# A third residual buffer, and routing of the next tile begun at the tile's first four tokens with its selection dealt out over 21 fours

## The chip, the cores and the metric

The kernel runs on one core of one Trainium2 chip, in one launch. The metric is device time in microseconds; a run's time is that of the whole program. The kernel before took 4234.45 us (median of 3 runs, 4230.75 to 4238.12).

## The reference

One inference step of a streaming encoder of one layer, with 1024 prompt rows and 8 x 16 sample rows of width 1024, all fp32. Two head groups of attention, an output projection, then a retrieval feed-forward over 16384 single-neuron experts (PEER). The change touches the last only:

```
def peer_block(xb):                                       # 128 tokens, 8 heads
    q  = (xb @ w_query).reshape(128, 8, 2, 128)
    s  = einsum('thpd,hpkd->thpk', q, sub_keys)           # two halves of 128 keys per head
    sv, si = top_k(s, 16)                                 # best 16 of each half
    cand = sv[:, :, 0, :, None] + sv[:, :, 1, None, :]    # 16 x 16 sums
    cidx = si[:, :, 0, :, None] * 128 + si[:, :, 1, None, :]
    fv, fi = top_k(cand.reshape(...), 16)                 # best 16 sums of a head
    eidx = take_along_axis(cidx, fi)                      # 8 x 16 = 128 experts a token
    g = softmax(fv)
    a = einsum('thkd,td->thk', expert_u[eidx], xb)
    w = g * gelu(a)
    return einsum('thk,thkd->td', w, expert_v[eidx])
h = h + peer(rms_norm(h, norm2_g));  y = rms_norm(h, norm_f_g)
```

## The kernel before

The program has two stages. The first does the attention of nine tiles of 128 rows (eight of the prompt, one of the samples) and leaves the residual rows h in a scratch tensor in HBM. The second, from about 1.1 ms on, is the feed-forward, and the change lies wholly in it.

**One token at a time.** A tile's experts are fetched token by token: the 128 experts of one token are one gather of 128 rows (partitions) x 2048 floats, u and v side by side, 1 MB, issued by GpSimd (L1040) into a ring of ten buffers. GpSimd issues gathers of four buffers when the four tokens that held them have been weighed (semaphore `four_used`, L1039). There are 32 "fours" in a tile, numbered f = 0 to 31.

**What a four does.** TensorE spreads the token's normed row over all partitions into PSUM (`spread_x`, L1264, from split bf16 rows x3, two tokens ahead of the dots). VectorE multiplies the u half with it and sums (`dot`, L1120), giving 128 scores. After four dots ScalarE takes one gelu (L1099) and multiplies with the gates (L1105). TensorE then weighs the v halves, accumulating in two PSUM banks over the whole tile (`weigh`, L1276). Then GpSimd issues four more gathers.

**Routing of the next tile** runs inside the current tile's fours, cut into steps that tables place: `PE_AT`, `ACT_AT` and `DVE_AT` (L59 to L76) give for each four the steps of TensorE, ScalarE and VectorE; each engine runs its queue strictly in that order, so a step that waits holds what is behind it. The steps of tile t + 1:

- norm: ScalarE squares the residual rows in `hb` and takes the root (L1050 to L1054), VectorE inverts it (L120 on) and forms x2 (L1139).
- split: VectorE cuts x2 into three bf16 parts (L1144 to L1152); SP copies these in 12 DMAs to x3 (L993).
- x2T: TensorE transposes x2 (L1288), ScalarE copies it out.
- q (k, l), k and l from 0 to 3: TensorE, 8 block products each (L1298); ScalarE copies four of them at once (L1061).
- keys (k): TensorE (L1307), then ScalarE's copy of the scores (L1069).
- halves (k, l): VectorE, the best 16 of 128 (`top16`, L1123); sums (k); best (k, h): the best 16 of 50 sums; experts (k, h): the expert numbers (L1193 to L1203). In all 16 + 4 + 8 + 8 steps a tile, the "selection".
- shift, gates, turn, turned: softmax of the gates, and the transposed lists that GpSimd and ScalarE read.

On TensorE the first step of a four stands amid the four's spreads and the others behind its weighing (L1325 to L1335). On VectorE the i-th step of a four stands behind its i-th dot. ScalarE's steps stand ahead of the four's gelu.

**End of a tile**, inside the next one: collect (VectorE adds PSUM to `hb`, at four 1; weighing waits for it), squares (ScalarE, L1079, at four 2), finish (VectorE, L1226, at four 3). SP then stores the block, waits for that, loads the block after next into the same one of two `hb` buffers (L996 to L1007), and goes on to the copies of the split rows (`spread`, L987).

Of the kernel before, what the change touches and what calls it, by code (L numbers as in the profile page):

```python
# [55 lines left out]
COLLECT_AT, SQUARES_AT, FINISH_AT = 1, 2, 3  # L56
# [3 lines left out]
PE_AT = {5: [("x2T",)], 23: [("turn",)], 14: [("keys", 3)]}  # L60
for k in range(4):
    PE_AT.setdefault(6 + 2 * k, [])
    if k:
        PE_AT[6 + 2 * k] += [("keys", k - 1)]
    PE_AT[6 + 2 * k] += [("q", k, 0), ("q", k, 1)]
    PE_AT[7 + 2 * k] = [("q", k, 2), ("q", k, 3)]
ACT_AT = {4: [("norm",)], 6: [("x2T",)], 8: [("q", 0)], 9: [("keys", 0)], 10: [("q", 1)], 11: [("keys", 1)],
          12: [("q", 2)], 13: [("keys", 2)], 14: [("q", 3)], 15: [("keys", 3)], 22: [("gates",)], 24: [("turned",)]}
ACT_ORDER = [s for f in sorted(ACT_AT) for s in ACT_AT[f]]
DVE_AT = {4: [("norm",)], 6: [("split",)], 21: [("shift",)], 22: [("gates",)], 24: [("turned",)]}  # L70
for k in range(4):
    pieces = [("halves", k, l) for l in range(4)] + [("sums", k), ("best", k, 0), ("best", k, 1)]
    pieces += [("experts", k, 0), ("experts", k, 1)]
    for i in range(3):
        DVE_AT[9 + 3 * k + i] = pieces[3 * i:3 * i + 3]
# [62 lines left out]
def build(nc, ins, outs):  # L138
# [6 lines left out]
    with ctx:  # L145
        def sem(name):
            return ctx.enter_context(nc.semaphore(name))
# [753 lines left out]
        hb = [carve(D) for _ in range(2)]  # L901
# [16 lines left out]
        c_left = carve(CAND)  # L918
# [18 lines left out]
        h_in = [sem(f"h_in{p}") for p in range(2)]  # L937
# [40 lines left out]
        with nc.Block() as block:  # L978

            @block.sync  # L980
            def _(sp):
                sp.dma_start(hb[0], h_dram[0:P, :]).then_inc(h_in[0], 16)
                sp.dma_start(g2_bc, g2[0:1, :].broadcast_to([P, D])).then_inc(bc_in, 16)
                sp.dma_start(gf_bc, gf[0:1, :].broadcast_to([P, D])).then_inc(bc_in, 16)
                sp.dma_start(hb[1], h_dram[P:2 * P, :]).then_inc(h_in[1], 16)

                def spread(t):  # L987
                    sp.wait_ge(split_ready, 3 * t + 3)
                    if t >= 2:
                        sp.wait_ge(xb_ready, SLOTS * (t - 1))  # L990
                    for c in range(3):
                        for g in range(4):
                            sp.dma_start(x3[t % 2][32 * c:32 * c + 32, g, :], parts3[c][32 * g:32 * g + 32, :])\  # L993
                              .then_inc(x3_in[t % 2], 16)

                def store(t):  # L996
                    sp.wait_ge(y_ready, t + 1)
                    sp.dma_start(y_p[t * P:(t + 1) * P, :] if t < NT_PROMPT else y_s, hb[t % 2]).then_inc(y_stored, 16)

                spread(0)  # L1000
                for t in range(NT):
                    if t >= 1:
                        store(t - 1)
                        if t + 1 < NT:
                            sp.wait_ge(y_stored, 16 * t)
                            sp.dma_start(hb[(t + 1) % 2], h_dram[(t + 1) * P:(t + 2) * P, :])\
                              .then_inc(h_in[(t + 1) % 2], 16)  # L1007
                    if t + 1 < NT:
                        spread(t + 1)
                store(NT - 1)  # L1010
                sp.wait_ge(y_stored, 16 * NT)

# [97 lines left out]
            def _(dve):  # L1110
# [22 lines left out]
                def route(t, step, k=0, h=0):  # L1133
                    p = t % 2
                    hs = slice(QSP * k, QSP * (k + 1))
                    if step == "norm":
                        dve.wait_ge(rms2_ready, t + 1)
                        invert_rms(dve, ch, rstd2[:, 0:1], ss2[:, 0:1], newton2, D)
                        dve.scalar_tensor_tensor(out=x2, in0=hb[p], scalar=rstd2[:, 0:1], in1=g2_bc,  # L1139
                                                 op0=ALU.mult, op1=ALU.mult).then_inc(x2_ready, 1)  # L1140
                    if step == "split":
# [4 lines left out]
                        if t >= 2:  # L1146
                            dve.wait_ge(ssf_ready, t - 1)
# [73 lines left out]
                def collect(t):  # L1221
                    dve.wait_ge(four_used, FOURS * (t + 1))
                    dve.tensor_tensor(hb[t % 2], PS[:, ACC:ACC + 2, :].rearrange("p a b -> p (a b)"), hb[t % 2], ALU.add)\
                       .then_inc(acc_free, 1)

                def finish(t):  # L1226
# [3 lines left out]
                    dve.scalar_tensor_tensor(out=hb[t % 2], in0=hb[t % 2], scalar=rstd2[:, 1:2], in1=gf_bc,  # L1230
# [22 lines left out]
            def _(pe):  # L1253
# [68 lines left out]
                for t in range(NT):  # L1322
                    for f in range(FOURS):
# [4 lines left out]
                        for step, *k in steps[:1]:  # L1328
                            route(t + 1, step, *k)
# [4 lines left out]
                        for step, *k in steps[1:]:  # L1334
                            route(t + 1, step, *k)  # L1335
# [63 lines left out]
```

## Time and profile before

| | us |
|---|---|
| runs, median of 3 | 4234.45 |
| profiled execution | 4222.83 |
| its span, first to last instruction | 4221.0 |
| TensorE busy | 2997.1 (71%) |
| VectorE busy | 2380.9 (56%) |
| ScalarE busy | 731.7 (17%) |
| GpSimd busy | 1181.9 (28%) |
| gathers, share of the 16 DMA engines over the span | 70.6% |

The shares are means over two unlike stages. In the second stage the slices of the page show DMA at 9 or 8 tenths nearly throughout and between 350 and 422 GB/s. To see what a four costs, the trace is cut at the gelus: stretch f of a tile runs from the start of the gelu of four f to that of four f + 1, and so holds the weighing of four f and the dots of four f + 1. DMA share is the mean busy share of the core's 16 DMA engines. The granted clock of TensorE is given as a share of 2.4 GHz.

### The profile page before, as it was taken

Reading aid. Unit: us, or ns where it says so; the run is one execution under the profiler, and the core shown is the slowest. Engines: PE = TensorE matmul, PEld = TensorE weight load, DVE = VectorE, ACT = ScalarE, POOL = GpSimd, SP = SyncE. Lnnn points to the kernel's source line nnn. Section 1 sums busy time; section 2 is a strip of 40 time slices with the busy share of each in tenths; the row PEclk is TensorE's granted clock in tenths of the full one; section 3 lists DMA queues with packets and bytes.
Section 4 is the critical chain, followed back from the end, with each engine's and each line's share of the span. In section 5 each row is a group of like instructions: output and inputs, shape, how many; then the busy total and the mean of one; then the engine's idle time right before and its main releaser. Section 6 shows DMA issues by size and latency. Waiting matters only on the chain.

```text
span 4221.0 us, 39656 instructions
## 1 busy us (share of the span) xinstructions
PE 2997.1 (71%) x13023; PEld 1218.1 (29%) x13023; DVE 2380.9 (56%) x6206; ACT 731.7 (17%) x2364; POOL 1181.9 (28%) x1330
## 2 busy tenths in 40 slices
PE   8999999996376666667657666666766765766665
PEld 4555555575041132123114113112311311311111
DVE  2333333324668469558657756855865774684544
ACT  2333333311111111111111111111111111111111
POOL 1001000000223333333432333333333333233332
PEclk9999999957587687777668768767767866877676
DMA  4000000231699999998999999999899999999998
GB/s 177 10 10 10 15 15 19 72 134 33 253 372 379 422 392 365 414 396 357 409 405 369 391 421 371 367 422 394 350 413 402 366 400 422 368 372 421 421 422 350
DMA packets 193573, 1276.81 MB, mean 302 GB/s; under 512 B 22640, under 2 KB 26608, under 8 KB 44528
## 3 DMA queue, kind: packets, MB, share of 16 engines
q0 software_dynamic: 165888, 1208.03, 70.6%
q1 hardware_dynamic: 27504, 66.63, 4.5%
q8 instruction: 81, 1.33, 0.1%
q14 instruction: 100, 0.82, 0.1%
HBM read 1255.17 MB, written 12.32 MB: 300 GB/s over the span
## 4 chain that ended last, share of the span: by engine, by line
DMA 28%; DVE 16%; PE 16%; issue 8%; ACT 4%; POOL 4%; DVEq 0%; POOLq 0%; SPq 0%; ACTq 0%
DMA arena<-in_experts,arena 25%; PE PS L1276 12%; DVE arena L1120 6%; POOL arena L1040 4%; ACT arena L1105 3%; PE PS L1298 3%; DVE arena L1198 1%; DVE arena L1195 1%; DVE arena L1201 1%; DMA out<-arena 1%; DMA arena<-h_scratch 1%; PE PS L1264 1%; DVE arena L1131 1%; DVE arena L1126 1%; DVE arena L1129 1%
## 5 line engine op out<-in xcount | busy, mean ns | idle before, releaser
L1120 DVE CUSTOM_DVE_ANT_0 arena<-arena,PS 128x1024 f32<-128x1024 f32 x1152 | 1393.1, 1220 | 999.5 <-DMA arena<-in_experts,arena 544.4
L1040 POOL DMA_INDIRECT arena<-in_experts,arena x1152 | 1106.3, 960 | 2090.6 <-PE PS L1276 1728.9
L1264 PE MATMUL PS<-arena 96*128 96x512 bf16 x2304 | 831.1, 468 | 983.4 <-DVE arena L1120 978.9
L1276 PE MATMUL PS<-arena 128*32 128x512 f32 x4608 | 955.0, 974 | 75.2 <-ACT arena L1105 35.5
L1264 PEld LDWEIGHTS PS<-arena 96*128 96x128 bf16 x2304 | 170.7, 105 | 1712.4 <-DVE arena L1120 1374.4
L1099 ACT ACTIVATE arena<-arena 128x4 f32<-128x4 f32 x288 | 59.2, 205 | 2405.1 <-DVE arena L1120 2395.9
L1276 PEld LDWEIGHTS PS<-arena 128*32 128x32 f32 x4608 | 166.8, 153 | 662.6 <-issue 384.4
L1298 PEld LDWEIGHTS PS<-arena 128*128 128x128 f32 x2304 | 291.6, 205 | 95.8 <-issue 88.5
L1298 PE MATMUL PS<-arena 128*128 128x128 f32 x2304 | 304.6, 291 | 1.1 <-ACT arena L1057 1.1
L739 PE MATMUL PS<-arena 128*128 128x512 f32 (+1 forms) x720 | 290.0, 556 | 3.8 <-ACT arena L471 2.9
L1105 ACT ACTIVATE arena<-arena 128x1 f32<-128x1 f32 x1152 | 244.9, 283 | 9.6
L422 POOL COPY arena<-arena 128x512 f32<-128x512 f32 x36 | 22.2, 616 | 687.4 <-POOLq L111 685.8
L739 PEld LDWEIGHTS PS<-arena 128*128 128x128 f32 x720 | 134.4, 192 | 132.7 <-issue 129.4
L719 PE MATMUL PS<-ident,arena 128*128 128x128 f32 x741 | 129.2, 306 | 45.5 <-ACT arena L521 24.2
L606 DVE TENSOR_TENSOR arena<-PS,arena 128x256 f32<-128x256 f32 x64 | 27.2, 424 | 197.2 <-PE PS L767 195.0
L811 PE MATMUL PS<-arena 128*128 128x512 f32 x288 | 129.1, 607 | 11.8 <-DVE arena L582 11.8
L521 ACT ACTIVATE arena<-arena 128x256 f32<-128x256 f32 (+1 forms) x128 | 85.6, 669 | 250.0 <-DVE arena L612 250.0
L719 PEld LDWEIGHTS PS<-ident,arena 128*128 128x128 f32 x741 | 98.9, 161 | 74.4 <-issue 30.7
L791 PE MATMUL PS<-arena 128*128 128x128 f32 (+1 forms) x640 | 100.3, 311 | 0.0
L610 DVE CUSTOM_DVE_ANT_0 arena<-arena 128x256 f32<-128x256 f32 (+1 forms) x128 | 83.8, 655 | 24.7 <-DVEq L111 24.7
L125 DVE TENSOR_SCALAR arena<-arena 128x1 f32<-128x1 f32 (+1 forms) x36 | 7.2, 199 | 156.3 <-ACT arena L1053 70.4
L1120 DVE DVE_READ_ACCUMULATOR2_ANT arena<- 128x1 f32 x1152 | 94.9, 82 | 0.0
(168 smaller groups left out, 2146.4 us busy)
## 6 DMA issues: line engine op xcount, KB each, us to landing
arena<-in_experts,arena POOLq DMA_INDIRECT x1152
arena<-in_w_in SPq DMA_DIRECT2D x4, 2048.0 KB, 16.0
arena<-in_w_query SPq DMA_DIRECT2D x8, 1024.0 KB, 5.7
arena<-arena SPq DMA_DIRECT2D x108, 64.0 KB
h_scratch<-arena SPq DMA_DIRECT2D x9, 512.0 KB, 2.6
arena<-h_scratch SPq DMA_DIRECT2D x9, 512.0 KB, 7.8
out<-arena SPq DMA_DIRECT2D x9, 512.0 KB, 8.0
arena<-in_x_prompt SPq DMA_DIRECT2D x8, 512.0 KB, 3.9
```

Source lines behind the costliest of these rows:

```text
L521: act.activation(sc[n % 2][:, 0:w], sc[n % 2][:, 0:w], ACT.Exp, bias=nm[:, n:n + 1], accum_out=den[:, n:n + 1]).then_inc(e_ready, 1)
L610: ch.mark(dve.tensor_tensor_reduce(s, s, bias, 1.0, floor, ALU.add, ALU.max, m_sb[:, n:n + 1]))
L719: return pe.transpose(PS[:, bank, k * P:(k + 1) * P], src, ident)
L739: mm = pe.matmul(PS[:, UNIT, 0:w], xT[:, j, :], w_in_sb[:, j, 512 * c:512 * c + w], start=(j == 0), stop=(j == KD - 1))
L791: mm = pe.matmul(PS[:, OA_BANK, cols], pT[n % 2][:, k, :], v_win[:, k, cols], start=(k == 0), stop=(k == A_BLK - 1))
L811: mm = pe.matmul(PS[:, 6 + c, :], oT[:, k, :], w_out_sb[:, k, 512 * c:512 * c + 512], start=(k == 0), stop=(k == KD - 1))
L1040: pool.indirect_dma_start(out=uv[r], out_offset=None, in_=experts, in_offset=bass.IndirectOffsetOnAxis(ap=expert_T[t % 2][:, tok:tok + 1], ...
L1105: act.activation(wz[n % 2][:, g, 31:32], a_gelu[n % 2][:, g:g + 1], ACT.Copy, scale=gate_T[t % 2][:, tok:tok + 1]).then_inc(wgt_ready, 1)
L1120: dve.tensor_tensor_reduce(uv[r][:, 0:D], uv[r][:, 0:D], xb(n), 1.0, 0.0, ALU.mult, ALU.add, a_dot[(n // 4) % 2][:, n % 4:n % 4 + 1]).then ...
L1264: mm = pe.matmul(PS[:, 2 + 2 * (n % 2) + c, :], pick[0:96, j:j + 1].broadcast_to([96, P]), x3[t % 2][0:96, g, 512 * c:512 * c + 512], star ...
L1276: mm = pe.matmul(PS[32 * g:32 * g + 32, ACC + c, :], wz[n % 2][:, g, 31 - f:63 - f], uv[r][:, D + 512 * c:D + 512 * c + 512], start=(f == ...
L1298: mm = pe.matmul(PS[:, Q_BANK, l * P:(l + 1) * P], w_query_sb[:, j, c:c + P], x2T[:, j, :], start=(j == 0), stop=(j == KD - 1))
```

## The change

There are three residual buffers instead of two; the load of a block is issued two tiles ahead. On SP the copies of the split rows stand ahead of the store. Routing starts at four 0 (norm), 1 (split, transposes) and 2 (first products). The products of a k come at fours 2 + 5k and 3 + 5k, the scores at 4 + 5k, always behind the weighing. ScalarE copies the products at 4 + 5k and the scores at 5 + 5k. VectorE's 36 selection steps are dealt by fixed lengths over fours 5 to 25, an experts step directly behind its best step. Squares move to four 4, finish to four 5. The squares' scratch is x2 instead of the score buffer, with another wait; one small scratch shares a buffer.

```
-COLLECT_AT, SQUARES_AT, FINISH_AT = 1, 2, 3
+COLLECT_AT, SQUARES_AT, FINISH_AT = 1, 4, 5
-PE_AT = {5: [("x2T",)], 23: [("turn",)], 14: [("keys", 3)]}
+PE_AT = {1: [("x2T",)], 27: [("turn",)]}
+ACT_AT = {0: [("norm",)], 2: [("x2T",)], 26: [("gates",)], 28: [("turned",)]}
 for k in range(4):
-    PE_AT.setdefault(6 + 2 * k, [])
-    if k:
-        PE_AT[6 + 2 * k] += [("keys", k - 1)]
-    PE_AT[6 + 2 * k] += [("q", k, 0), ("q", k, 1)]
-    PE_AT[7 + 2 * k] = [("q", k, 2), ("q", k, 3)]
-ACT_AT = {4: [("norm",)], 6: [("x2T",)], 8: [("q", 0)], 9: [("keys", 0)], 10: [("q", 1)], 11: [("keys", 1)],
-          12: [("q", 2)], 13: [("keys", 2)], 14: [("q", 3)], 15: [("keys", 3)], 22: [("gates",)], 24: [("turned",)]}
+    PE_AT[2 + 5 * k] = [("q", k, 0), ("q", k, 1)]
+    PE_AT[3 + 5 * k] = [("q", k, 2), ("q", k, 3)]
+    PE_AT[4 + 5 * k] = [("keys", k)]
+    ACT_AT[4 + 5 * k] = [("q", k)]
+    ACT_AT[5 + 5 * k] = [("keys", k)]
-DVE_AT = {4: [("norm",)], 6: [("split",)], 21: [("shift",)], 22: [("gates",)], 24: [("turned",)]}
-for k in range(4):
-    pieces = [("halves", k, l) for l in range(4)] + [("sums", k), ("best", k, 0), ("best", k, 1)]
-    pieces += [("experts", k, 0), ("experts", k, 1)]
-    for i in range(3):
-        DVE_AT[9 + 3 * k + i] = pieces[3 * i:3 * i + 3]
+SELECT_AT, SELECT_FOURS = 5, 21
+STEP_LENGTH = {"halves": 4, "sums": 6, "best": 3, "experts": 6}
+SELECTION = []
+for k in range(4):
+    SELECTION += [("halves", k, l) for l in range(4)]
+    SELECTION += [("sums", k), ("best", k, 0), ("experts", k, 0), ("best", k, 1), ("experts", k, 1)]
+DVE_AT = {0: [("norm",)], 1: [("split",)]}
+select_length = sum(STEP_LENGTH[s[0]] for s in SELECTION)
+before = 0
+for s in SELECTION:
+    DVE_AT.setdefault(SELECT_AT + before * SELECT_FOURS // select_length, []).append(s)
+    before += STEP_LENGTH[s[0]]
+DVE_AT[SELECT_AT + SELECT_FOURS - 1].append(("shift",))
+DVE_AT[SELECT_AT + SELECT_FOURS] = [("gates",)]
+DVE_AT[28] = [("turned",)]
...
-        hb = [carve(D) for _ in range(2)]
+        hb = [carve(D) for _ in range(3)]
-        c_left = carve(CAND)
+        c_left = s_left[:, 0:CAND]
...
                 spread(0)
                 for t in range(NT):
+                    if t + 1 < NT:
+                        spread(t + 1)
                     if t >= 1:
                         store(t - 1)
-                        if t + 1 < NT:
+                        if t + 2 < NT:
                             sp.wait_ge(y_stored, 16 * t)
-                            sp.dma_start(hb[(t + 1) % 2], h_dram[(t + 1) * P:(t + 2) * P, :])\
-                              .then_inc(h_in[(t + 1) % 2], 16)
-                    if t + 1 < NT:
-                        spread(t + 1)
+                            sp.dma_start(hb[(t + 2) % 3], h_dram[(t + 2) * P:(t + 3) * P, :])\
+                              .then_inc(h_in[(t + 2) % 3], 16)
...
                 def squares(t):
                     act.wait_ge(acc_free, t + 1)
-                    act.wait_ge(halves_done, 4 * min(t + 2, NT))
-                    act.activation(s_flat, hb[t % 2], ACT.Square, accum_out=ss2[:, 1:2]).then_inc(ssf_ready, 1)
+                    act.wait_ge(split_ready, 3 * min(t + 3, NT))
+                    act.wait_ge(x2T_psum, min(t + 3, NT))
+                    act.activation(x2, hb[t % 3], ACT.Square, accum_out=ss2[:, 1:2]).then_inc(ssf_ready, 1)
...
                     if step == "split":
-                        if t >= 2:
-                            dve.wait_ge(ssf_ready, t - 1)
...
                         spread_x(4 * n + 2)
                         spread_x(4 * n + 3)
-                        for step, *k in steps[:1]:
-                            route(t + 1, step, *k)
                         spread_x(4 * n + 4)
                         spread_x(4 * n + 5)
                         weigh(n, 0)
                         weigh(n, 1)
-                        for step, *k in steps[1:]:
+                        for step, *k in steps:
                             route(t + 1, step, *k)
```

The dealing gives VectorE these steps of the selection, k / l or h:

```
four  5 halves 0/0 0/1      four 12 sums 1                  four 19 best 2/1, experts 2/1
four  6 halves 0/2 0/3      four 13 best 1/0, experts 1/0   four 20 halves 3/0
four  7 sums 0, best 0/0    four 14 best 1/1, experts 1/1   four 21 halves 3/1 3/2
four  8 experts 0/0         four 15 halves 2/0              four 22 halves 3/3, sums 3
four  9 best 0/1, exp. 0/1  four 16 halves 2/1 2/2          four 23 best 3/0
four 10 halves 1/0 1/1      four 17 halves 2/3, sums 2      four 24 experts 3/0, best 3/1
four 11 halves 1/2 1/3      four 18 best 2/0, experts 2/0   four 25 experts 3/1
```

## Rows read from the trace of the kernel before

**Rows 1.** Head of the page.
```profile
span 4221.0 us, 39656 instructions
```

**Rows 2.** Tiles 0, 4, 8: length; busy PE, PEld, DVE, ACT, POOL; clock; DMA share; GB/s.
```profile
1111.90:1454.40 342.50, 232.89 (x1064) 75.22 (x1064) 226.94 (x576) 45.84 (x179) 123.68 (x128) 0.74 0.98 393
...
2499.20:2849.10 349.90, 230.17 (x1066) 72.55 (x1066) 229.66 (x584) 49.81 (x184) 123.33 (x128) 0.73 0.97 390
...
3895.00:4206.60 311.60, 199.39 (x742) 35.73 (x742) 155.41 (x256) 36.63 (x161) 110.59 (x118) 0.69 1.00 415
```

**Rows 3.** The same of tile 4: its stretches 3-5, 6-7, 8-13, 14-21, 22-31.
```profile
2529.90:2564.60 34.70, 19.53 (x95) 6.08 (x96) 19.91 (x35) 8.07 (x21) 11.76 (x12) 0.71 0.95 386
2564.60:2588.90 24.30, 16.82 (x109) 8.89 (x106) 9.84 (x16) 2.72 (x12) 7.50 (x8) 0.91 1.02 365
2588.90:2668.50 79.60, 60.90 (x361) 33.28 (x361) 61.32 (x201) 9.50 (x37) 23.26 (x24) 0.82 0.89 355
2668.50:2748.30 79.80, 50.61 (x192) 9.50 (x192) 71.48 (x220) 11.77 (x44) 30.48 (x31) 0.67 0.96 383
2748.30:2849.10 100.80, 63.52 (x242) 11.42 (x242) 49.35 (x81) 10.71 (x52) 39.08 (x42) 0.69 1.01 421
```

**Rows 4.** The same of single stretches: vector-bound, the two behind it, a quiet one.
```profile
2720.10:2732.50 12.40, 6.51 (x24) 1.15 (x24) 11.99 (x25) 1.02 (x6) 4.61 (x4) 0.64 0.97 388
2732.50:2740.70 8.20, 6.67 (x25) 1.26 (x26) 4.89 (x10) 1.10 (x6) 2.51 (x3) 0.66 0.97 381
2740.70:2748.30 7.60, 5.59 (x24) 1.10 (x24) 5.46 (x11) 3.89 (x8) 3.39 (x5) 0.77 1.00 417
...
2788.10:2798.00 9.90, 6.21 (x24) 1.12 (x24) 4.92 (x8) 1.02 (x5) 3.75 (x4) 0.67 1.02 423
```

**Rows 5.** Timeline of a quiet four: start, us, engine, line, operation, idle before.
```profile
2789.20 3.62 PE L1276 MATMUL PS<-arena 128*32 128x512 f32 x16
...
2792.75 1.04 PE L1264 MATMUL PS<-arena 96*128 96x512 bf16 x4
...
2793.13 0.94 POOL L1040 DMA_INDIRECT arena<-in_experts,arena  x1 [5.41 <-PE PS L1276]
```

**Rows 6.** Timeline around the norm step of tile 4.
```profile
2531.58 0.35 SPq L1006 DMA_DIRECT2D arena<-h_scratch  x1
...
2539.37 1.06 ACT L1051 ACTIVATE arena<-arena 128x1024 f32<-128x1024 f32 x1 [8.38 <-DMA arena<-h_scratch]
2540.54 1.28 ACT L1053 ACT_TABLE_LOAD   x1
...
2542.14 1.28 ACT L1099 ACT_TABLE_LOAD   x1
2542.16 0.15 DVE L125 TENSOR_SCALAR arena<-arena 128x1 f32<-128x1 f32 x1 [8.93 <-ACT arena L1053]
```

**Rows 7.** Timeline of TensorE and VectorE: two product blocks behind a weighing, twice.
```profile
2590.01 3.64 PE L1276 MATMUL PS<-arena 128*32 128x512 f32 x16
2593.59 4.35 PE L1298 MATMUL PS<-arena 128*128 128x128 f32 x32
...
2599.75 1.22 DVE L1120 CUSTOM_DVE_ANT_0 arena<-arena,PS 128x1024 f32<-128x1024 f32 x1 [3.98 <-issue]
...
2616.01 3.17 PE L1276 MATMUL PS<-arena 128*32 128x512 f32 x16 [0.31 <-ACT arena L1105]
...
2623.82 1.22 DVE L1120 CUSTOM_DVE_ANT_0 arena<-arena,PS 128x1024 f32<-128x1024 f32 x1 [2.23 <-PE PS L1264]
```

**Rows 8.** Timeline: scores on TensorE, their copy, first and last operation of a selection.
```profile
2583.86 1.13 PE L1307 MATMUL PS<-arena 128*128 128x128 f32 x8
...
2642.62 0.56 ACT L1069 COPY arena<-PS 128x512 f32<-128x512 f32 x1
...
2591.24 0.29 DVE L1124 MAX8 arena<-arena 128x8 f32<-128x128 f32 x1
...
2592.63 0.28 DVE L1131 FIND_INDEX8 arena<-arena 128x8 uint32<-128x128 f32 x1
```

More of the change, by code:

```diff
@@ L936, in build @@
         bc_in = sem("bc_in")
-        h_in = [sem(f"h_in{p}") for p in range(2)]
+        h_in = [sem(f"h_in{p}") for p in range(3)]
         rank_ready = sem("rank_ready")
@@ L984, in _ @@
                 sp.dma_start(gf_bc, gf[0:1, :].broadcast_to([P, D])).then_inc(bc_in, 16)
-                sp.dma_start(hb[1], h_dram[P:2 * P, :]).then_inc(h_in[1], 16)
+                for t in range(1, 3):
+                    sp.dma_start(hb[t], h_dram[t * P:(t + 1) * P, :]).then_inc(h_in[t], 16)
                 def spread(t):
@@ L997, in store @@
                     sp.wait_ge(y_ready, t + 1)
-                    sp.dma_start(y_p[t * P:(t + 1) * P, :] if t < NT_PROMPT else y_s, hb[t % 2]).then_inc(y_stored, 16)
+                    sp.dma_start(y_p[t * P:(t + 1) * P, :] if t < NT_PROMPT else y_s, hb[t % 3]).then_inc(y_stored, 16)
                 spread(0)
                 for t in range(NT):
+                    if t + 1 < NT:
+                        spread(t + 1)
                     if t >= 1:
                         store(t - 1)
-                        if t + 1 < NT:
+                        if t + 2 < NT:
                             sp.wait_ge(y_stored, 16 * t)
-                            sp.dma_start(hb[(t + 1) % 2], h_dram[(t + 1) * P:(t + 2) * P, :])\
-                              .then_inc(h_in[(t + 1) % 2], 16)
-                    if t + 1 < NT:
-                        spread(t + 1)
+                            sp.dma_start(hb[(t + 2) % 3], h_dram[(t + 2) * P:(t + 3) * P, :])\
+                              .then_inc(h_in[(t + 2) % 3], 16)
                 store(NT - 1)
@@ L1049, in route @@
                     if step == "norm":
-                        act.wait_ge(h_in[p], 16 * (t // 2) + 16)
-                        act.activation(x2, hb[p], ACT.Square, accum_out=ss2[:, 0:1]).then_inc(ss2_ready, 1)
+                        act.wait_ge(h_in[t % 3], 16 * (t // 3) + 16)
+                        act.activation(x2, hb[t % 3], ACT.Square, accum_out=ss2[:, 0:1]).then_inc(ss2_ready, 1)
                         act.wait_ge(ss2_ready, t + 1)
@@ L1138, in route @@
                         invert_rms(dve, ch, rstd2[:, 0:1], ss2[:, 0:1], newton2, D)
-                        dve.scalar_tensor_tensor(out=x2, in0=hb[p], scalar=rstd2[:, 0:1], in1=g2_bc,
+                        dve.scalar_tensor_tensor(out=x2, in0=hb[t % 3], scalar=rstd2[:, 0:1], in1=g2_bc,
                                                  op0=ALU.mult, op1=ALU.mult).then_inc(x2_ready, 1)
@@ L1222, in collect @@
                     dve.wait_ge(four_used, FOURS * (t + 1))
-                    dve.tensor_tensor(hb[t % 2], PS[:, ACC:ACC + 2, :].rearrange("p a b -> p (a b)"), hb[t % 2], ALU.add)\
+                    dve.tensor_tensor(hb[t % 3], PS[:, ACC:ACC + 2, :].rearrange("p a b -> p (a b)"), hb[t % 3], ALU.add)\
                        .then_inc(acc_free, 1)
@@ L1229, in finish @@
                     ch.restart()
-                    dve.scalar_tensor_tensor(out=hb[t % 2], in0=hb[t % 2], scalar=rstd2[:, 1:2], in1=gf_bc,
+                    dve.scalar_tensor_tensor(out=hb[t % 3], in0=hb[t % 3], scalar=rstd2[:, 1:2], in1=gf_bc,
                                              op0=ALU.mult, op1=ALU.mult).then_inc(y_ready, 1)
```

## The prediction

> **What bounds the kernel now.** Times in the profile are of one execution: span 4221.0 us, execution 4222.8 us, 11.6 us under the median of the three runs, 4234.45 [rows 1]. I forecast for the profiled execution and add 11.6 at the end.
>
> I read the slices of the page first (the DMA line is at 8 or 9 from the twelfth on: the expert stage), then stretches cut at the tiles. A tile with routing of the next one in it takes 342.5 us (the first), then seven tiles from 1454.4 to 3895.0, a mean of 348.7. The last tile, which routes nothing, needs 311.6 us for 31 of its 32 fours and runs at 415 GB/s [rows 2]. So the gathers of expert rows are the floor, and routing puts some 25 us per tile on top. The reader is to see in [rows 3] where: one tile cut at the gelus of its fours (stretch f runs from the gelu of four f to that of four f+1). In a quiet four the DMA share is 1.01, 423 GB/s, 9.9 us [rows 4], so 32 fours are 316.8 us. Stretches 6 and 7 take 24.3 us at share 1.02 but 365 GB/s: the twelve copies that make the split token rows are then in the DMA engines, which costs 24.3 - 19.8 = 4.5 us. Store and load of a residual block, 1.05 MB at 423 GB/s, are 2.5 us. Floor: 316.8 + 4.5 + 2.5 = 323.8. Above it tile 4 (349.9) loses 26.1: 1.0 in stretches 0 to 2 (the 30.7 us that the others leave); 34.7 - 29.7 - 2.5 = 2.5 in 3 to 5; 79.6 - 59.4 = 20.2 in 8 to 13, where the projection is on TensorE and the DMA share falls to 0.89; 0.6 in 14 to 21; 1.8 in 22 to 31. The mean tile loses 348.7 - 323.8 = 24.9.
>
> How much lateness is free? Four gathers are issued when the weighing matmuls of a four end, 5 us after its gelu (gelu 2788.10, weighing 2789.20, its follower 2792.75, first issue 2793.13) [rows 4, 5]. A four that comes late starves the DMA only once it has eaten the transfers still queued. When the consumer was the brake and then is let go, it catches up by what lay ready: after the last vector-bound stretch (2720.10, 12.4 us) the next two take 8.2 and 7.6 instead of 9.9, together 4.0 us [rows 4]. So up to about 4.0 us of lateness costs nothing, and what exceeds it is lost for good. This is my main tool: I follow lateness L from four to four, and cut it at 4.0.
>
> **The change part by part.**
>
> *Third buffer, norm moved from four 4 to four 0.* Before, the load of the next residual block is issued at 2531.58, after the store of the old one, and ScalarE's Square starts only at 2539.37; VectorE waits 8.93 us for the norm and its dots stand still [rows 6]. With a third buffer the block is there four fours earlier. Of the 18.1 us stretch only 2.5 us were lost (above), since the ring covered the rest. Late next: at four 0 the norm's Square, table load and root (2.7 us, [rows 6]) start after the last weights, 1.0 us behind the gelu, so VectorE has them at 3.8; its own part, six steps on one column and a pass, is under two dots' time (2.4), so it is through at 6.2, with 9.9 - 6.2 = 3.7 us for the three dots left: nothing lost. On SP the copies of the split rows now go ahead of the store; the store waits for the finish at four 5 anyway, so nothing is late there.
>
> *Split and collect at four 1.* behind one dot (over at 2.4) VectorE adds collect and the split, five passes over 128x1024 at a dot's 1.2 or less: 8.4 with them, 12.0 with the three dots left, instead of 9.9: L = 2.1, gone in the next four, which can do 9 us where the data's pace is 12.15 (next sentence but one). The scratch of the final squares goes to another buffer and its wait is on steps long done: nothing. The twelve copies move with the split to about fours 2 and 3; their 4.5 us stay, and slow the data there, so pace is 12.15 in these two.
>
> *Projection spread out.* The same matmuls: two blocks behind the weighing of fours 2+5k and 3+5k, keys behind 4+5k (k = 0 to 3). Before, fours 6 to 13 had two blocks each, one of them often amid the spreads. The price of two blocks behind a weighing stands in the trace: weighing from 2590.01, 32 matmuls from 2593.59 for 4.35, third dot of the next four at 2599.75; in a second case weighing 2616.01, third dot 2623.82 [rows 7]. Gelu to weighing 1.1, weighing to third dot 7.8 or 9.7, two more dots 2.4: the next four takes 11.3 to 13.3; I take the middle, 12.3 (A). There are eight A: fours 3, 4, 8, 9, 13, 14, 18, 19.
>
> *Squares at four 4.* ScalarE now has there the copy of a projection (ready at 1.1 + 3.6 + 4.3 = 9.0, copied by 9.7 to 10.3) and behind it Square, two table loads and a root, 2539.37 to 2543.42 = 4.05 us in the old place [rows 6]; so gelu of four 4 comes at 14.3 (13.2 to 15.4) instead of 12.3. The trace shows the two table loads at 1.28 us each with 0.1 us or less around them [rows 6].
> The Trainium skill ("ScalarE: Activation LUTs", What ACT_TABLE_LOAD costs) puts a drain of 1.38 us to each switch beside the same 1.28. By that the gelu would be 2.8 us later and seven tiles lose some 19 us more (time 4214); the rows show no such drain, so the sum is by the rows.
>
> *The keys' wait: what the change adds.* The scores leave TensorE behind the weighing of four 4+5k, ScalarE copies them, and VectorE's first selection step stands behind the first dot of four 5+5k. The wait blocks the other three dots, and with them gelu, weighing, gathers. Gelu to weighing 1.1, weighing 3.6 [rows 5], keys 1.1, copy 0.56 [rows 8], hand-offs: scores at 6.5 to 7.2. Then a selection of 1.7 (2591.24 to 2592.91 [rows 8]), dot 1.2, selection, two dots: 13.7 to 14.4; I take 14.0 (B) for fours 5 and 10. Fours 15 and 20 hold a single selection: 12.2 (B'). Before, the keys of the first head pair were scored in mid-four, earlier than VectorE wanted them, so no row shows this wait; from below its price is that of other fours, 9.9.
>
> *Selection over 21 fours.* VectorE's work is the same; before, three of twelve fours were vector-bound (12.4 us with 11.99 busy [rows 4]). A best and two experts steps are 11.99 - 4.92 = 7.1 there; with the best step no dearer than a selection (1.7, below), one of each is 4.4. Now a four has no more than these: 4.9 + 4.4 = 9.3, below 9.9. But the vector-bound stretches 14 to 21 had lost only 0.6 net, because they end in catching up. A four with two selections and no new wait takes 4.9 + 3.4 + 0.2 = 8.5; one with a sums step, which I take for no longer than two selections, 7.9 (weighing over at 4.7, spread 0.8 of the 1.04 for two tokens [rows 5], two dots) to 9.0. In these lateness is given back.
>
> *The walk.* Four 1: L 2.1. Four 2: 0. Four 3: 12.3 - 12.15, L 0.2. Four 4: 14.3 - 9.9, L 4.6, lost 0.6. Four 5: B against 11.15 (the store and load are now in 5 and 6): lost 2.85. Four 6 (8.5 against 11.15): L 1.35; 7: 0; 8: 2.4; 9: 4.8, lost 0.8; 10: B, lost 4.1; 11: 2.6; 12: 0.6; 13: 3.0; 14: lost 1.4; 15: B', lost 2.3; 16: 2.7; 17: 1.8; 18: lost 0.2; 19: lost 2.4; 20: lost 2.3; then L goes back to 0 and the rest is as before, its 2.8 included (stretches 0 to 2 and 22 to 31). Sum 17.0 + 2.8 = 19.8 per tile against 24.9: 5.1 us over seven tiles = 36. The first tile, with no store and no squares, had lost 342.5 - 321.3 = 21.2 and loses 19.8 by the same walk: 1.4. The last tile and the prologue (same order of steps; the third load lies under it) stay. Total 37: 4222.8 - 37 = 4186, and with 11.6 4197, rounded to **4195**.
>
> With A at 11.3 and B at 13.7 the walk loses 8.7 + 2.8 = 11.5 per tile: 102 us less, 4132. With A 13.3, squares 15.4, B 14.4: 26.5 + 2.8 = 29.3, 40 us more, 4274.
>
> **The rivals.**
> *The ring covers it all.* If lateness in the pairs and the key waits never passes 4.0 us (because the fours without steps between them give more back than I say), only the 2.8 stay: 7 x 22 + 18 = 172 us less, 4062; half of that, 4150 or under, is in reach. For it: the turn step had the same shape before (TensorE behind a weighing, VectorE waiting a four later), and the ten stretches 22 to 31 that hold it take 100.8 us, 1.8 over the pace [rows 3]. Against: that is one wait with quiet fours around it; here a B comes behind two A.
> *The key wait decides: slower.* Place: first selection of each head pair, four times a tile. My gain of 5.1 us per tile is gone when A and B together are 5.1 us dearer in the fours in which L stands at 4.0, that is when the scores come some 1.3 us later than 6.7 at all four places (a late end of the block matmuls, ScalarE's copy behind it, blocks run at the lower of TensorE's two levels, 1.2 GHz: the granted clock was 0.82 in stretches 8 to 13 and 0.67 to 0.71 where TensorE has less to do [rows 3]). At the upper ends: 4274. For it: VectorE did not have this wait before; against: fours 6 and 7, 11 and 12 give back 3 to 4 us each.
> *A draw.* The transfers are hidden anyway: what is lost in fours 3 to 5 was 2.5, and the projection costs the same wherever it lies, so 4234.
>
> **How the numbers follow.** Forecast (part of the loss goes, 4132 to 4225) 0.56; ring covers more, below 4132: 0.10; within 0.2% (8.5 us, about what a measurement of this kernel tells from no change) 0.12; slower through the key wait 0.22. So faster 0.66, same 0.12, slower 0.22. The range runs from 4125 to 4270, the two ends of A and B, and leaves out some of the cover rival and of the worst key wait; the forecast's own range is 4132 to 4225.
>
> **What would show it.** VectorE's norm wait of 8.93 us gone. Tiles at about 343 us. Stretches of 12 us at fours 3, 8, 9, 13, 14, 18, 19, of 14 at 4, 5, 10, 12 at 15 and 20, and 8 to 9 at 6, 7, 11, 16, 21. VectorE's first selection (L1124) waiting 4 to 6 us for ScalarE's key copy (L1069), 32 times. No stretch with VectorE busy above 10 us. Wrong: tiles under 335 or over 349; key copy long done when VectorE comes; DMA share below 0.9 in a place not named here.

## The result and the profile after

The changed kernel takes **4107.19 us** (median of 4 runs, 4092.34 to 4108.21) against 4232.60 us before in the same session: ratio 0.9695, 95% interval 0.967 to 0.972. The forecast was 4195, and its range began at 4125. The direction was right, the gain more than three times the one forecast.

The head of the page after (profiled execution 4107.32 us):

```profile
span 4105.5 us, 39648 instructions
```

Stretches of the changed kernel, columns as in [rows 2]: tiles 0, 3 and 8, then tile 3 cut as in [rows 3] (stretches 0-2, 3-5, 6-7, 8-13, 14-21, 22-31).

```profile
1113.20:1440.70 327.50, 231.60 (x1067) 72.75 (x1068) 225.47 (x576) 46.64 (x179) 122.34 (x128) 0.75 1.01 414
2106.86:2437.22 330.36, 231.45 (x1066) 72.22 (x1066) 229.57 (x584) 50.49 (x184) 122.51 (x129) 0.75 1.01 412
3778.90:4091.00 312.10, 200.29 (x742) 35.52 (x742) 155.41 (x256) 36.66 (x160) 110.76 (x118) 0.68 0.99 412
...
2106.86:2142.43 35.57, 25.53 (x112) 8.79 (x112) 19.35 (x29) 4.18 (x16) 11.34 (x13) 0.68 1.02 385
2142.43:2177.86 35.43, 22.59 (x112) 7.98 (x112) 22.61 (x64) 8.25 (x22) 10.22 (x11) 0.80 0.99 401
2177.86:2197.94 20.08, 16.46 (x80) 6.26 (x80) 15.85 (x49) 2.12 (x11) 8.55 (x10) 0.75 1.00 412
2197.94:2259.78 61.84, 46.74 (x248) 18.96 (x248) 49.08 (x137) 8.10 (x34) 23.27 (x24) 0.81 1.01 413
2259.78:2337.71 77.93, 54.69 (x272) 18.51 (x272) 62.34 (x192) 10.23 (x44) 31.42 (x32) 0.80 1.01 417
2337.71:2437.22 99.51, 65.43 (x242) 11.72 (x242) 60.33 (x116) 17.61 (x60) 37.70 (x40) 0.67 1.01 422
```

Seven tiles from 1440.70 to 3778.90 have a mean of 334.0 us where they had 348.7, so 10.2 above the floor of 323.8 instead of 24.9; the first went from 342.5 to 327.5, and the last, which routes nothing, stayed at 312 [rows 2]. Together 7 x 14.7 + 15.0 = 118, the whole difference of the two profiled executions but for 2 us. Stretches 8 to 13 took 79.6 us at DMA share 0.89 [rows 3] and take 61.84 at 1.01, with 248 matmuls in them where there were 361.

Single stretches of tile 3: with squares and blocks (3), the first key wait (4), the second (9), the third (14), the fourth (19), and two with blocks (7, 8).

```profile
2142.43:2156.18 13.75, 9.89 (x58) 4.90 (x58) 6.66 (x16) 5.56 (x12) 3.76 (x4) 0.88 1.02 422
...
2156.18:2169.55 13.37, 6.56 (x30) 1.93 (x30) 8.14 (x25) 1.64 (x6) 3.75 (x4) 0.78 1.01 414
...
2208.81:2220.73 11.92, 5.69 (x32) 1.86 (x32) 7.82 (x25) 1.65 (x6) 3.75 (x4) 0.90 1.02 423
...
2259.78:2270.06 10.28, 6.12 (x32) 1.88 (x32) 6.32 (x17) 1.65 (x7) 3.76 (x4) 0.81 1.01 420
2310.78:2321.05 10.27, 6.12 (x32) 1.88 (x32) 6.31 (x17) 1.64 (x7) 3.76 (x4) 0.82 1.01 421
...
2186.15:2197.94 11.79, 9.41 (x56) 4.98 (x56) 8.08 (x13) 1.06 (x6) 4.92 (x6) 0.85 1.01 424
2197.94:2208.81 10.87, 9.27 (x56) 4.80 (x56) 8.88 (x21) 1.64 (x6) 3.87 (x4) 0.85 1.02 424
```

(The prediction's four f+1 is stretch f.) Forecast for stretches 4, 9, 14 and 19 were 14.0, 14.0, 12.2 and 12.2. Only the first came out so. The timelines of stretch 4 and then of stretch 9 show why: gelu, weighing, scores, their copy, and VectorE's first selection operation with its wait.

```profile
2156.18 0.21 ACT L1111 ACTIVATE arena<-arena 128x4 f32<-128x4 f32 x1
...
2157.32 3.39 PE L1286 MATMUL PS<-arena 128*32 128x512 f32 x16 [2.36 <-ACT arena L1117]
...
2161.84 0.59 ACT L1080 COPY arena<-PS 128x512 f32<-128x512 f32 x1 [4.57 <-PE PS L1317]
...
2162.57 0.29 DVE L1136 MAX8 arena<-arena 128x8 f32<-128x128 f32 x1 [4.75 <-DVEq L121]
...
2208.81 0.21 ACT L1111 ACTIVATE arena<-arena 128x4 f32<-128x4 f32 x1 [2.31 <-DVE arena L1132]
...
2209.96 1.92 PE L1286 MATMUL PS<-arena 128*32 128x512 f32 x16 [0.52 <-ACT arena L1117]
...
2213.01 0.59 ACT L1080 COPY arena<-PS 128x512 f32<-128x512 f32 x1 [3.10 <-PE PS L1317]
...
2213.75 0.29 DVE L1136 MAX8 arena<-arena 128x8 f32<-128x128 f32 x1 [3.83 <-DVEq L121]
```

The same sixteen weighing matmuls take 3.39 us in the one and 1.92 in the other. Two fours of blocks lie ahead of both. But in stretch 4 the gelu came late, behind the squares on ScalarE, and TensorE had stood still for 2.36 us just before its weighing. TensorE's granted clock over the two weighings (the third number from the right) is 0.56 and 1.00, that is mostly 1.2 GHz in the one and 2.4 GHz in the other:

```profile
2157.32:2160.71 3.39, 3.39 (x17) 0.66 (x17) 0.51 (x1) 0.00 (x0) 0.00 (x0) 0.56 1.00 418
2209.96:2211.88 1.92, 1.92 (x17) 0.48 (x17) 0.00 (x0) 0.00 (x0) 0.00 (x0) 1.00 1.00 418
```

The first tile, in which no squares stand ahead of that gelu, shows that this pause is what differs: its stretch 4 (from 1161.07) takes 11.9 us like stretch 9, with this weighing, and so does that of the first tile in e4 and in e11.

```profile
1162.21 1.92 PE L1286 MATMUL PS<-arena 128*32 128x512 f32 x16 [0.51 <-ACT arena L1117]
```

In stretches 9, 14 and 19 of tiles 0 to 7, 21 of 24 weighings take 1.92 us, the other three 3.41 to 3.51. In stretch 9 of tile 3 VectorE begins 4.94 us after the gelu, in stretch 4 6.39; I had put the scores at 6.5 to 7.2 everywhere. The wait itself is there, as a row of VectorE's waits says (us in total, times, longest).

```profile
DVE arena L1136 <- DVEq L121: 135.0, 34, 10.7
```

Four of the 34, the longest among them, lie ahead of the first tile; the other 30 are 3.1 to 5.9 us each. The row names VectorE's own queue, but in both timelines above VectorE begins 0.14 to 0.15 us after ScalarE's copy of the scores ends.

### The profile page after: what moved, and what is told of

Its sections match the earlier page's. It is cut to its first block and busy times, and to the rows that moved or that the text cites. A ratio compares the mean times of both kernels' runs of the same rounds, so it can differ in the third digit from the quotient of the medians.

```text
span 4105.5 us, 39648 instructions
## 1 busy us (share of the span) xinstructions
PE 3021.5 (74%) x13023; PEld 1210.3 (29%) x13023; DVE 2376.4 (58%) x6206; ACT 735.8 (18%) x2363; POOL 1176.5 (29%) x1330
## 3 DMA queue, kind: packets, MB, share of 16 engines
q8 instruction: 81, 1.33, 0.1%
## 5 line engine op out<-in xcount | busy, mean ns | idle before, releaser
L1274 PE MATMUL PS<-arena 96*128 96x512 bf16 x2304 | 842.8, 470 | 825.4 <-DVE arena L1132 789.8
L1308 PEld LDWEIGHTS PS<-arena 128*128 128x128 f32 x2304 | 282.0, 203 | 93.6 <-issue 92.1
L1308 PE MATMUL PS<-arena 128*128 128x128 f32 x2304 | 294.6, 289 | 1.1 <-ACT arena L1068 1.1
L749 PEld LDWEIGHTS PS<-arena 128*128 128x128 f32 x720 | 134.3, 192 | 132.4 <-issue 129.1
L1136 DVE MAX8 arena<-arena 128x8 f32<-128x128 f32 (+1 forms) x216 | 57.1, 265 | 144.9 <-DVEq L121 135.0
L821 PE MATMUL PS<-arena 128*128 128x512 f32 x288 | 129.1, 607 | 11.8 <-DVE arena L592 11.8
```

The source lines that it names most:

```text
L749: mm = pe.matmul(PS[:, UNIT, 0:w], xT[:, j, :], w_in_sb[:, j, 512 * c:512 * c + w], start=(j == 0), stop=(j == KD - 1))
L821: mm = pe.matmul(PS[:, 6 + c, :], oT[:, k, :], w_out_sb[:, k, 512 * c:512 * c + 512], start=(k == 0), stop=(k == KD - 1))
L1274: mm = pe.matmul(PS[:, 2 + 2 * (n % 2) + c, :], pick[0:96, j:j + 1].broadcast_to([96, P]), x3[t % 2][0:96, g, 512 * c:512 * c + 512], star ...
L1308: mm = pe.matmul(PS[:, Q_BANK, l * P:(l + 1) * P], w_query_sb[:, j, c:c + P], x2T[:, j, :], start=(j == 0), stop=(j == KD - 1))
```

## The experiments

Twelve runs were made, of ten new kernels (e12 repeats e7) and of the changed one once more (e11), in three sessions, each beside runs of the kernel before. "Tile" is the mean of tiles 1 to 7 in the one profiled execution of each.

| version | us (median, range) | ratio to before (95%) | tile us |
|---|---|---|---|
| e1 before + third buffer | 4211.97 (4202.05-4215.37) | 0.9934 (0.9910-0.9958) | 345.7 |
| e8 before + selection dealt out | 4119.27 (4107.34-4121.96) | 0.9728 (0.9697-0.9759) | 334.2 |
| e10 before + both of these | 4095.11 (4093.18-4098.46) | 0.9670 (0.9647-0.9693) | 331.2 |
| e2 after, selection crammed | 4304.56 (4298.66-4311.86) | 1.0158 (1.0132-1.0184) | 358.0 |
| e3 after, no key wait | 4118.91 (4106.80-4125.66) | 0.9728 (0.9705-0.9750) | 333.4 |
| e9 after, no key wait, order by hand | 4110.06 (4087.02-4120.77) | 0.9708 (0.9657-0.9759) | 332.6 |
| e4 after, blocks one four earlier | 4173.29 (4161.99-4182.33) | 0.9849 (0.9820-0.9879) | 340.8 |
| e5 after, ring of nine | 4126.95 (4113.93-4140.34) | 0.9741 (0.9711-0.9772) | 338.2 |
| e6 after, first step amid the spreads | 4093.62 (4092.64-4096.83) | 0.9670 (0.9646-0.9693) | 331.0 |
| e7 after, one block per four | 4093.59 (4084.65-4094.50) | 0.9666 (0.9639-0.9694) | 330.8 |
| e12 the same again | 4095.46 (4094.52-4095.95) | 0.9672 (0.9653-0.9691) | 331.1 |
| e11 after again | 4104.10 (4099.43-4115.71) | 0.9696 (0.9673-0.9720) | 334.0 |

### Which part of the change did it

**e1**, the third buffer alone (`hb` of three, loads two tiles ahead), norm and projection in their old places.

> The kernel before with the third residual buffer alone: three blocks, loads two tiles ahead, all tables and the order on SP as before. Theory (ring): lateness up to 4 us per episode is covered by the gathers under way, so of the 8.93 us norm wait only the 2.5 us above the pace were lost; those go: tiles 1 to 7 from 348.7 to about 346, time about 4212 (4205 to 4220). VectorE's norm wait falls from 8.93 us to under 3. Rival (the buffer is the gain): the wait was lost in full, tiles at about 340 or below, time 4150 or below.

26 us, as expected, and VectorE's longest wait for the norm is 1.3 us; the first row below is tile 4, the second its stretch 3, 18.1 us before with the norm wait of [rows 6] in it.

```profile
2510.50:2856.20 345.70, 234.55 (x1066) 74.20 (x1066) 230.25 (x584) 49.75 (x183) 123.91 (x128) 0.73 0.97 394
2540.40:2552.80 12.40, 6.65 (x25) 1.09 (x25) 6.96 (x15) 4.96 (x11) 3.90 (x4) 0.64 1.02 424
```

**e8**, the dealing alone:
```
-        DVE_AT[9 + 3 * k + i] = pieces[3 * i:3 * i + 3]
+SELECT_AT, SELECT_FOURS = 9, 17
...     # dealt out by STEP_LENGTH as in the change; shift 25, gates 26, turn 27, turned 28
```

> The kernel before with its selection dealt out over seventeen fours (nine to twenty-five) instead of twelve, all else in its old place, so still two buffers and the projection in fours 6 to 13. Theory (the selection crammed behind the two blocks cost 20 us a tile, and dealing alone gives part of it back): stretches 8 to 13 fall from 79.6 to 68 to 73, tiles to 338 to 343, time 4150 to 4200. Rival (the gain came from spreading the projection, and dealing alone is worth nothing, since blocks in every four leave no four to catch up in): tiles 347 to 349, time 4225 to 4240.

Well better than either theory: 115.6 us, of the change's 125 to 132. Tile 3 and its stretches 8 to 13:

```profile
2120.51:2453.88 333.37, 229.87 (x1066) 73.87 (x1066) 230.36 (x584) 49.81 (x183) 123.14 (x128) 0.74 1.00 408
2210.55:2277.24 66.69, 54.72 (x360) 32.30 (x360) 53.20 (x177) 9.49 (x36) 23.28 (x24) 0.89 1.01 417
```

TensorE does in them what it did before, 360 matmuls in six fours, in 66.69 us instead of 79.60 [rows 3].

**e10**, e8 with e1's buffer.

> The kernel before with the third buffer and the selection dealt over seventeen fours, the projection left in fours 6 to 13. Theory (the two gains are in different fours and add up; spreading the projection out is worth nothing): stretch 3 falls to 12.4 as with the buffer alone, tiles 331 to 332, 2.5 us less than with the dealing alone, time about 4100 (4085 to 4112). Rival (spreading the projection is a part of the gain of its own, so that only all three reach 4107): tiles 334 to 337, time 4115 to 4135.

The two add up (26 and 115.6 against 140.7 us together), and the projection in its old place is no handicap: 4095 against 4104 to 4107 for the changed kernel. e10 differs from that kernel in more than the place of the projection, in the order on TensorE and the place of the squares too; but e6 below, which spreads the projection out and goes back to the old order on TensorE, ends at 4094. Spreading the projection out was worth nothing in time here.

**e2**, the opposite cut: the changed kernel with three selection steps in each of three fours per head pair.
```
-    DVE_AT.setdefault(SELECT_AT + before * SELECT_FOURS // select_length, []).append(s)
...
+        DVE_AT[SELECT_AT + 5 * k + i] = SELECTION[9 * k + 3 * i:9 * k + 3 * i + 3]
```

> The changed kernel with its selection packed again as before: three steps in each of three fours per head pair (fours 5-7, 10-12, 15-17, 20-22), none in the others; all else as changed. Theory (VectorE's dealing frees the fours in which the ring recovers): fours 6, 7 of each pair take 10 and 12.4 us instead of 8.3, lateness is not given back, 15 to 30 us more per tile: 4230 to 4340. Rival (TensorE's spreading out is the gain, the dealing is idle detail): 4107 to 4130.

67 us slower than before. The third buffer and the spread projection without the dealing lose. Its stretch 9 in tile 3, and the next:

```profile
2302.99:2316.62 13.63, 6.12 (x32) 1.89 (x32) 9.39 (x33) 1.64 (x6) 3.74 (x4) 0.74 0.98 383
2316.62:2326.49 9.87, 7.10 (x24) 1.27 (x24) 9.26 (x45) 1.06 (x5) 3.76 (x4) 0.67 0.70 261
```

The four behind the key wait is itself full (VectorE 9.26 of 9.87 us), so nothing is caught up and the DMA share falls to 0.70.

### Why the key wait was cheaper than forecast

**e4** takes the blocks of pairs 1 to 3 one four away from the keys, all else as in the change.
```
-    PE_AT[2 + 5 * k] = [("q", k, 0), ("q", k, 1)]
-    PE_AT[3 + 5 * k] = [("q", k, 2), ("q", k, 3)]
+    early = 1 if k else 0
+    PE_AT[2 + 5 * k - early] = [("q", k, 0), ("q", k, 1)]
+    PE_AT[3 + 5 * k - early] = [("q", k, 2), ("q", k, 3)]
```

> The changed kernel with the product blocks of head pairs 1 to 3 one four earlier (fours 6, 7, 11, 12, 16, 17), so that a four without blocks stands ahead of the four whose weighing the scores follow. Theory (clock): in the changed kernel the weighing ahead of the scores takes 1.9 us at the full granted clock, since TensorE was busy with blocks in the two fours ahead; here it takes 3.4 to 3.6 us at half, the scores come at 6.4 to 6.9 us after the gelu instead of 4.9, stretches 9, 14, 19 take 13.6, 12, 12 us instead of 12, 10.3, 10.3; time about 4150 (4125 to 4165). Rival (the wait is short for another reason, the clock does not matter): weighing and stretches as in the changed kernel, time 4100 to 4120.

Stretches 9, 14 and 19 rose to 13.1, 11.7 and 11.9 (means), near the prices of the prediction, and the kernel to 4173, 8 us above the end of this run's range. Stretch 9 of tile 3, and in it the gelu, weighing, copy of the scores, and first selection:

```profile
2242.43:2255.67 13.24, 7.45 (x32) 2.06 (x32) 7.89 (x25) 1.64 (x7) 3.75 (x4) 0.76 1.01 420
```
```profile
2242.43 0.21 ACT L1112 ACTIVATE arena<-arena 128x4 f32<-128x4 f32 x1 [7.59 <-DVE arena L1133]
...
2243.57 3.25 PE L1287 MATMUL PS<-arena 128*32 128x512 f32 x16
...
2247.95 0.59 ACT L1081 COPY arena<-PS 128x512 f32<-128x512 f32 x1 [4.43 <-PE PS L1318]
...
2248.69 0.29 DVE L1137 MAX8 arena<-arena 128x8 f32<-128x128 f32 x1 [5.08 <-DVEq L122]
```

13.24 - 11.92 = 1.32 us of stretch for 3.25 - 1.92 = 1.33 us of weighing: with a four of other work between, the stretch's granted clock is 0.76 instead of 0.90, and the scores are late by just that. The time of the kernel is not the price of these waits alone: of the 6.8 us by which its tiles are longer than the changed kernel's, the three stretches hold 3.5, and the stretches of the blocks, moved with them, about as much.

**e3** begins the selection one four later (`SELECT_AT, SELECT_FOURS = 6, 20`), so no wait for scores is left.

> The changed kernel with the selection dealt over fours 6 to 25 instead of 5 to 25, so that the scores are ready a whole four before VectorE asks for them. Theory (the key wait is what is left): stretches 4, 9, 14, 19 fall from 13.8, 12.2, 10.5, 10.5 to some 8 to 9, or to 11.5 where two blocks stand ahead; lost time per tile from 10 to about 5.5 us; tiles at 329, time about 4066 (4050 to 4080). Rival (the ring covers the wait, it costs nothing): 4100 to 4115.

My theory failed: stretches 9, 14 and 19 fell to 8.9, 8.8 and 9.0 as it wanted, but the time did not, since the stretches with blocks grew from 11.3-12.7 to 12.7-13.2 (means) and took the gain back. There was little to gain, too: tiles of 333.4 us stand 2.4 us above the 331 at which three other schedules end below. With the new deal VectorE does other steps while the blocks run. **e9** tests whether that is why these stretches grew. It keeps the wait away too, and by hand puts one experts step, or none, beside the blocks, never the `best` steps (chains of passes of 0.2 us over 50 columns).
```
+    h0, h1, h2, h3, su, b0, e0, b1, e1 = SELECTION[9 * k:9 * k + 9]
+    DVE_AT[6 + 5 * k] = [h0, h1, h2]
+    DVE_AT[7 + 5 * k] = [h3, su, b0]
+    DVE_AT[8 + 5 * k] = [e0]
+    DVE_AT[10 + 5 * k] = [b1, e1]
```

> The kernel after with the selection steps of each head pair put by hand: the score halves in the two fours behind the key copy, with the sums and the first best; an experts step in the first four with blocks of the next pair, none in the second, the second best and experts step in the four with its keys. So VectorE never waits for scores, and runs none of the small chained steps while blocks run. Theory (the small chained steps of VectorE make 32 block matmuls take 6.1 us to release instead of 4.3 to 4.7): stretches 7, 8, 12, 13, 17, 18 fall from the 13.0 to 13.3 of the version without a key wait to 11.3 to 12, tiles 330 to 333, time about 4090 (4070 to 4115). Rival (the blocks take longer because no key wait stands behind them, whatever VectorE does): these stretches stay at 12.8 to 13.3, tiles 338 to 343, time 4130 to 4175.

The stretches with blocks fell to 11.8-12.1 and 10.4-11.0, the time lies in the theory's range, below that of the rival. Of 48 pairs of blocks (tiles 0 to 7, six places) 43 in e3 took over 5.5 us from their first matmul to the release of the spread behind them, 8 in e9, and 4 in the changed kernel. Stretch 8 of tile 3 in e3, then in e9: blocks, copy of their products, the dot behind.

```profile
2207.68 3.84 PE L1308 MATMUL PS<-arena 128*128 128x128 f32 x32
...
2213.78 0.59 ACT L1072 COPY arena<-PS 128x512 f32<-128x512 f32 x1 [9.64 <-remote]
2213.92 1.22 DVE L1132 CUSTOM_DVE_ANT_0 arena<-arena,PS 128x1024 f32<-128x1024 f32 x1 [4.15 <-issue]
```
```profile
2204.42 3.84 PE L1310 MATMUL PS<-arena 128*128 128x128 f32 x32
...
2208.29 0.59 ACT L1074 COPY arena<-PS 128x512 f32<-128x512 f32 x1 [5.78 <-PE PS L1310]
...
2209.09 1.22 DVE L1134 CUSTOM_DVE_ANT_0 arena<-arena,PS 128x1024 f32<-128x1024 f32 x1 [5.43 <-PE PS L1276]
```

The record gives both 3.84 us, but the copy that waits for them comes 6.10 us after their first in e3 and 3.87 in e9. e9 changed two things at once, the kind of step and the amount of VectorE work beside the blocks; which of them it is, and how it reaches TensorE, stays open. The time shows less of it than the stretches: e3, e9 and the changed kernel lie within their scatter of each other.

### What lateness is free, and what is left

**e5** has `RING = 9` instead of 10.

> The kernel after with nine buffers in the gather ring instead of ten. Theory (late fours are free up to some 4.0 us because that much lies ready in the ring, and only the excess is lost): one gather of 2.5 us less lies ready, so 1.5 us are free; walking the measured stretches of the changed kernel with 1.5 instead of 4.0 loses some 8 us more per tile, tiles at about 342, time about 4172 (4150 to 4195). Rival (the ring is not what covers lateness, the stretches only add up on VectorE and TensorE): tiles stay at 334 to 336 and the time within 20 us of 4107.

Between the two. 4127 misses the theory's range and lies at the edge of the rival's 20 us; tiles are 4.2 us longer where the walk said 8, in an execution 13 us above the run's median. The ring does cover some lateness, but a gather less costs half of what cutting lateness at 1.5 us says, or less.

**e6** puts the first TensorE step of a four back amid the spreads (`steps[:1]` behind the second spread, `steps[1:]` behind the weighing).

> The kernel after with the first TensorE step of a four put back amid the four's spreads, as before the change: so one of two product blocks, or the keys, runs ahead of the weighing instead of behind it. Theory (what makes a four late is what stands behind its weighing): the scores are there before the gelu, stretches 9, 14, 19 fall to 8 to 9.5 and stretches with blocks to 9.5 to 10.5, tiles 327 to 331, time about 4075 (4060 to 4095). Rival (a block amid the spreads only makes the spreads late instead, and the first dots of the next four with them): stretches with blocks stay at 11 to 13, tiles 333 to 337, time 4100 to 4135.

**e7** has one block per four in fours 2 to 21 (`PE_AT[2 + 5*k + l] = [("q", k, l)]`, keys at 6 + 5k), the selection from four 8 on, and gates, turn and turned two fours later.

> The kernel after with one product block per four (fours 2 to 21, keys between the groups) instead of two in two fours and none in the next, and the selection four fours later so that it never waits for scores. Theory (a four is late by what stands behind its weighing on TensorE, and two blocks are 2 us too many while one fits): stretches with a block 9.5 to 10.2, none above 10.5 but the split and the squares, tiles 326 to 330, time about 4060 (4045 to 4085). Rival (with one block per four TensorE is too idle, its granted clock stays near half, and weighing and block together take as long as before): stretches with a block 10.5 to 11.5, tiles 340 or more, time 4145 to 4200.

Both land at 4094, and e10 at 4095: e6 inside its range, near the upper end; e7 9 us above its theory's range, and its tiles, at 330.8, a little above too, though its stretches from 6 to 21 take 9.5 to 10.5 in the mean. To compare e7 with the changed kernel itself, both ran once more side by side.

> The changed kernel itself, beside the version with one block per four on the same chip: 4107, tiles at 334.

> The version with one product block per four again, now beside the changed kernel itself: 4094, 0.3% under it, since the DMA engines stand idle 0.7 us per tile there against 3.7 us. Rival: the difference was the scatter of four runs, and both come within 5 us of each other.

4095.46 (4094.52 to 4095.95) against 4104.10 (4099.43 to 4115.71): the ranges don't touch, and one block per four is 0.2% faster than the change, a little less than expected. Tile 3 of e12, e6 and e10, a fence each:

```profile
2111.40:2441.70 330.30, 230.38 (x1067) 74.03 (x1068) 230.77 (x584) 50.50 (x184) 120.91 (x128) 0.76 1.01 411
```
```profile
2111.80:2441.70 329.90, 227.97 (x1066) 72.31 (x1066) 231.33 (x584) 49.73 (x183) 121.66 (x128) 0.75 1.01 412
```
```profile
2114.07:2445.94 331.87, 230.81 (x1066) 73.62 (x1066) 230.56 (x584) 49.78 (x183) 122.85 (x128) 0.74 1.00 410
```

Three different schedules, one tile length (mean 331.0 to 331.2), at a DMA share of 1.00 to 1.01. Counted from the packets in the traces, tiles 1 to 7 of e6, e10 and e12 have no moment without a transfer under way; the changed kernel has 0.8 us of such time per tile, the kernel before 5.4. So what is left is most likely the transfers themselves, and 331 a better floor than my 323.8. That is read from the traces and not tested: no run changes what is transferred.

## Why the prediction was wrong

The forecast was 79 us too high in the profiled execution: 7 x (343.6 - 334.0) = 67 in seven tiles, 341.1 - 327.5 = 14 in the first, less 2 in what lies around them. The prediction's own sign of being wrong, tiles under 335, came.

**The failed step is the price of "The keys' wait".** I put scores at 6.5 to 7.2 us after the gelu at all four places, with a weighing of 3.6 us from a quiet four, where the granted clock was 0.67 [rows 4, 5]. But at three of the four places TensorE goes from two fours of blocks into the weighing with pauses of 1 us or less (tile 3), its granted clock is 1.00, and the weighing takes 1.92; only at the first do the squares on ScalarE hold it up before. Measured stretches (means of tiles 1 to 6) are 13.8, 12.2, 10.5 and 10.5 for 14.0, 14.0, 12.2 and 12.2. Put into my own walk, these four alone bring it from 17.0 to 11.5 lost per tile: some 5.5 of the 9.6 us. The stretches with blocks, at 11.3 to 13.0 for 12.3, alone bring it to 14.0. With all measured stretches the walk loses 9.2, and 12.0 with the 2.8 that I left standing; the trace says 10.2. e4 shows the cause of the cheap wait by taking it away, and at waits near my prices its tiles are 6.8 us longer, half of it in these stretches.

These shares are the walk's and not measured, and they vary with the execution: in e11, the changed kernel once more, stretches 9, 14 and 19 take 12.4, 11.0 and 11.1 and those with blocks 11.0 to 12.1, and the walk gives 12.8 and 11.8 where it gave 11.5 and 14.0, at the same tile of 334.0. One error went the other way. To four 2 (stretch 1) I gave no lateness; with the twelve copies under way it took 13.2 us in the mean, for the 12.15 that I had worked out as the data's pace. By itself this adds 3.1 to the walk. Its row in tile 3:

```profile
2117.82:2130.38 12.56, 7.27 (x32) 2.16 (x32) 4.92 (x8) 2.07 (x7) 4.82 (x6) 0.77 1.03 339
```

**The second error was one of cause.** I read the loss of stretches 8 to 13 as the price of the projection on TensorE, took two blocks at 12.3 from rows in which selection steps ran beside them [rows 7], and gave the dealing credit only in fours without blocks. e8 and e10 leave the blocks where they were and have those stretches at about 66.7: the crammed selection was what cost. So the direction was right partly by luck: the projection, to which I charged the loss, could have stayed where it was, and the dealing pays nearly all. Why three selection steps in a four cost so much beside blocks stays open; e3 and e9 show only that the blocks' results come later with one deal of VectorE's steps than with another.

**What held.** The third buffer: 2.5 us per tile forecast, 2.9 measured in e1. Squares at four 4: 14.3 forecast, 13.75 in the row, 13.6 in the mean. The drain that the Trainium skill ("ScalarE: Activation LUTs", What ACT_TABLE_LOAD costs) adds to each table switch would have made it 17.1; the trace does not show it, as the root stands between the two loads with 0.02 us on either side:

```profile
2153.27 1.28 ACT L1096 ACT_TABLE_LOAD   x1
2154.57 0.29 ACT L1096 ACTIVATE arena<-arena,eps 128x1 f32<-128x1 f32 x1
2154.88 1.28 ACT L1111 ACT_TABLE_LOAD   x1
```

Selection fours without a wait at 7.9 to 9.0 (8.0 to 8.6 measured), a wait of some 4 us for the key copy at each of the four places, VectorE nowhere above 10 us in the stretches shown. The lateness rule held for the order of things and overstated the loss: by 1.8 us per tile above, by a factor of two in e5.

**The rivals.** "The ring covers it all" (4062) came nearer in time than my forecast. By my floor of 323.8 its mechanism fails, since tiles lose 10.2 us and not 2.8. By a floor of 331 it holds nearly: the changed kernel loses 3.0 us per tile there, e6 and e7, from whose tiles the 331 is read, have no key wait. Which floor is right decides between the two accounts, and with 331 my walk charges to lateness much of what is the transfers' own time. The slower case needed scores 1.3 us later than I assumed; at three places they came 1.8 us earlier than the 6.7 named there. A draw is out.

## What to carry to other kernels

Take an operation's duration from a row with the same work right before it: TensorE's weighing cost 3.6 or 1.9 us by what had gone ahead of it (a quiet four, or a pause of 2.4 us, against blocks with short pauses), and a wait behind it moved by that much. When a slow stretch holds two engines' work at once, don't charge it to one of them before a run has thinned out the other alone; here one list of VectorE steps, dealt evenly, was nearly the whole gain. And when different schedules end at the same time, look for what they share (here the DMA engines, at a share of 1.00 to 1.01) before moving steps again.

## What was not expected of the hardware

The recorded length of a run of matmuls, whose ends are modelled in these profiles, can hide 2 us. Thirty-two block matmuls show 3.84 us in e3 and in e9, with the products' copy 6.10 and 3.87 us after the first. In stretch 8 of e3 the weighing ahead takes 3.55 us, in that of e9 1.92, so the pairs also differ in the granted clock just before; but in e3 pairs that follow a weighing of 2.9 to 3.2 us are slow too, and in e9 many behind a weighing of 3.6 us are not. No run here says by what path.
